# Streaming expert weights with 16 KB rows: two ring slots filled by one transfer

## The reference

```python
logits = (xf @ w_router) + b_router          # 264 tokens, 32 experts
top_v, top_e = lax.top_k(logits, 4)
gates = jax.nn.softmax(top_v, axis=-1)
# for the tokens xb of every expert e:
gu = xb @ w_e1[e] + b_e1[e]                  # w_e1[e]: 1024 x 2048
g, u = gu[:, :1024], gu[:, 1024:]
g = jnp.minimum(g, 7.0); u = jnp.clip(u, -7.0, 7.0)
h = (u + 1.0) * (g * jax.nn.sigmoid(1.702 * g))
rows = h @ w_e2[e] + b_e2[e]                 # w_e2[e]: 1024 x 1024
# out = sum over a token's four experts of gate * rows
```

## Time and profile before

| | |
|---|---|
| median of 3 runs | 1284.78 us (1280.65 to 1286.63) |
| the profiled execution | 1283.03 us, span 1281.3 us |
| mean granted TensorE clock | 0.974 |
| TensorE matmuls | 1172.0 us, 91% of the span |
| TensorE weight loads | 569.3 us, 44% |
| VectorE, ScalarE, GpSimd | 335.5, 181.5, 28.3 us |
| moved by DMA | 457.41 MB, mean 357 GB/s |
| expert transfers of 1 MiB | 380 |

### The profile page before, as it was taken

How to read it: one execution, slowest core, us unless ns; L and a number is a source line. 1 busy time by engine, 2 the same in 40 slices (tenths; PEclk the granted TensorE clock), 3 DMA queues, 4 the chain that set the end, 5 groups by cost and what they waited for, 6 DMA issues and landing times.

```text
span 1281.3 us, 15118 instructions
## 1 busy us (share of the span) xinstructions
PE 1172.0 (91%) x5539; PEld 569.3 (44%) x5539; DVE 335.5 (26%) x805; ACT 181.5 (14%) x350; POOL 28.3 (2%) x58
## 2 busy tenths in 40 slices
PE   5999999699899999999999999989998999999996
PEld 3888888578333433333333333333332333232332
DVE  2397620815112121220212121212112021212123
ACT  3111512313001101111110101011110101010102
POOL 5000000200000000000000000000000000000000
PEclk9999999898889999999999999999999999999999
DMA  8449333796589999999999999999999999999994
GB/s 238 150 157 349 124 129 132 276 402 230 197 352 407 421 422 421 421 421 421 421 421 421 421 422 421 421 422 421 421 421 420 421 421 421 422 421 421 422 420 181
DMA packets 92470, 457.41 MB, mean 357 GB/s; under 512 B 7811, under 2 KB 36699, under 8 KB 43797
## 3 DMA queue, kind: packets, MB, share of 16 engines
q1 hardware_dynamic: 90528, 452.31, 87.9%
q10 hardware_dynamic: 1085, 3.01, 0.6%
q0 software_dynamic: 832, 1.76, 0.5%
HBM read 453.71 MB, written 3.81 MB: 357 GB/s over the span
## 4 chain that ended last, share of the span: by engine, by line
PE 52%; DMA 23%; SPq 13%; DVE 6%; issue 3%; ACT 2%; ACTq 0%; POOL 0%; DVEq 0%; POOLq 0%
DMA ring<-in_w_e 23%; PE ps L1495 15%; PE ps L1515 13%; SPq L351 12%; PE ps L1209 12%; PE ps L1225 3%; DVE ring L928 2%; PE ps L1457 1%; PE ps L1466 1%; PE ps L1409 1%; PE ps L1505 1%; DVE mix L1079 1%; DVE mix L1076 1%; DVE mix L1082 1%; SPq L359 1%
## 5 line engine op out<-in xcount | busy, mean ns | idle before, releaser
L1495 PE MATMUL ps<-ring,mix 128*64 128x512 f32 x2016 | 456.5, 598 | 26.6 <-DMA ring<-in_w_e 25.2
L1495 PEld LDWEIGHTS ps<-ring,mix 128*64 128x64 f32 x2016 | 134.2, 136 | 333.3 <-issue 237.5
L1515 PE MATMUL ps<-ring,mix 128*64 128x512 f32 x1024 | 240.6, 624 | 22.0 <-issue 11.0
L1076 DVE TENSOR_SCALAR mix<-ps 128x512 f32<-128x512 f32 x32 | 22.1, 692 | 603.2 <-PE ps L1495 603.2
L1515 PEld LDWEIGHTS ps<-ring,mix 128*64 128x64 f32 x1024 | 81.0, 143 | 160.8 <-issue 146.7
L1209 PE MATMUL ps<-xn,ring 128*128 128x264 f32 x384 | 89.9, 398 | 4.5 <-DVE xn L760 4.5
L1209 PEld LDWEIGHTS ps<-xn,ring 128*128 128x128 f32 x384 | 75.4, 197 | 18.1 <-issue 4.6
L687 ACT ACTIVATE mix<-mix 128x512 f32<-128x512 f32 x32 | 20.1, 630 | 417.3 <-DVE mix L1076 417.3
L1466 PEld LDWEIGHTS ps<-mix 128*128 128x128 f32 x544 | 64.9, 196 | 14.4 <-issue 13.0
L697 ACT ACTIVATE mix<-ps 64x512 f32<-64x512 f32 x64 | 37.8, 591 | 233.7 <-PE ps L1515 233.3
L1466 PE MATMUL ps<-mix 128*128 128x128 f32 x544 | 69.5, 282 | 1.3 <-ACT rstd L669 1.3
(11 more groups left out here) (281 smaller groups left out, 574.9 us busy)
## 6 DMA issues: line engine op xcount, KB each, us to landing
ring<-in_w_e SPq DMA_DIRECT2D x380, 1024.0 KB, 24.8
ring<-in_w_in SPq DMA_DIRECT2D x8, 1024.0 KB, 16.0
ring<-in_cache_mem_k SPq DMA_DIRECT2D x8, 1024.0 KB, 4.8
ring<-in_cache_mem_v SPq DMA_DIRECT2D x8, 1024.0 KB, 8.4
ring<-in_w_k SPq DMA_DIRECT2D x4, 1024.0 KB, 8.9
ring<-in_w_v SPq DMA_DIRECT2D x4, 1024.0 KB, 12.6
ring<-in_w_out SPq DMA_DIRECT2D x4, 1024.0 KB, 12.7
ring<-in_w_q SPq DMA_DIRECT2D x4, 1024.0 KB, 11.9
```

Of the source, the lines that this page charges most:

```text
L1076: dve.tensor_scalar(g1, ps[0][:, :], LIMIT, None, ALU.min).then_inc(S["g_clamped"], 1)
L1495: m = pe.matmul(ps[gu][CAP * i:CAP * i + CAP, :], xeT[:, k, CAP * e2:CAP * e2 + CAP], g_u[gu][:, 512 * i:512 * i + 512], start=False, stop ...
L1515: m = pe.matmul(ps[3][CAP * i:CAP * i + CAP, :], hTv[:, k % 4, CAP * (k // 4):CAP * (k // 4) + CAP], ring[:, s, D * (k % 2) + 512 * i:D * ...
```

## The change

One constant is new: `DEAL[k]` is the set of contraction rows that belong to block k, every second row of a group of 256. `fill` now takes two neighbouring slots s and s + 1 with one transfer of 2 MiB. For w_e1, partition p gets rows 256 (s/2) + 2p and the one after it, 16 KB in one piece; for w_e2, it gets four rows of 4 KB, again 16 KB. Only the even slots' semaphores are used, and the wait in front of a transfer is for the later of the two slots to be free. The head pieces take the rows of `DEAL[k]`, still in pieces of 4 KB. On TensorE, `gather` and L1559 read the token matrix at every second column, `turn_h` reads `hh` at every fourth, `up` waits for the even slot's semaphore, and `down` waits once for two slots.

```diff
+DEAL = [slice(2 * P * (_k // 2) + _k % 2, 2 * P * (_k // 2 + 1), 2) for _k in range(KD)]
 
                 sp.wait_ge(S["freed"], free)
                 if s < W_SLOTS:
-                    src = a["w_e1"][0][bass.ds(e, 1), s * P:(s + 1) * P, :].rearrange("o p c -> p (o c)")
-                    dst = ring[:, s, :]
+                    src = a["w_e1"][0][bass.ds(e, 1), s * P:(s + 2) * P, :].rearrange("o (p t) c -> p (o t c)", t=2)
                 else:
                     j = s - W_SLOTS
-                    src = a["w_e2"][0][bass.ds(e, 1), j * 2 * P:(j + 1) * 2 * P, :].rearrange(
-                        "o (p t) c -> p (o t c)", t=2)
-                    dst = ring[:, s, :]
+                    src = a["w_e2"][0][bass.ds(e, 1), j * 2 * P:(j + 2) * 2 * P, :].rearrange(
+                        "o (p t) c -> p (o t c)", t=4)
+                dst = ring[:, s:s + 2, :].rearrange("p s c -> p (s c)")
                 sp.dma_start(dst, src).then_inc(filled[s], 16)
 
             def expert(e, b, first=0):
 
-                for s in range(first, RING):
-                    fill(e, s, RING * b + freed_after(MOE0 + s - RING))
+                for s in range(first, RING, 2):
+                    fill(e, s, RING * b + freed_after(MOE0 + s + 1 - RING))
...
-                    sp.dma_start(head[k][gu], a["w_e1"][0, 0, k * P:(k + 1) * P, D * gu:D * gu + D]).then_inc(S["head_filled"], 16)
+                    sp.dma_start(head[k][gu], a["w_e1"][0, 0, DEAL[k], D * gu:D * gu + D]).then_inc(S["head_filled"], 16)
...
-            for s in range(HEAD_SLOTS, W_SLOTS):
-                fill(1, s, freed_after(MOE0 + 2 * (s - HEAD_SLOTS)))
+            for s in range(HEAD_SLOTS, W_SLOTS, 2):
+                fill(1, s, freed_after(MOE0 + 2 * (s + 1 - HEAD_SLOTS)))
...
-                            m = pe.matmul(ps[4 + i][:, P * (k % 4):P * (k % 4) + P], xnt[:, t, k * P:(k + 1) * P],
+                            m = pe.matmul(ps[4 + i][:, P * (k % 4):P * (k % 4) + P], xnt[:, t, DEAL[k]],
...
-                        pe.wait_ge(filled[k], 16 * b + 16 * (fills_before(MOE0 + k) - 1))
+                        pe.wait_ge(filled[k - k % 2], 16 * b + 16 * (fills_before(MOE0 + k) - 1))
                     else:
-                        pe.wait_ge(filled[k], 16 * b + 16 * fills_before(MOE0 + k))
+                        pe.wait_ge(filled[k - k % 2], 16 * b + 16 * fills_before(MOE0 + k))
...
-                    c = 2 * P * (j // 2) + j % 2
-                    m = pe.transpose(ps[2][:, j * P:(j + 1) * P], hh[:, c:c + 2 * P - 1:2], ident[:, :])
+                    m = pe.transpose(ps[2][:, j * P:(j + 1) * P], hh[:, j:4 * P:4], ident[:, :])
...
-                    if k % 2 == 0:
+                    if k % 4 == 0:
                         pe.wait_ge(filled[s], 16 * b + 16 * fills_before(MOE0 + s))
...
-                m = pe.transpose(ps[2][:, NB * k:NB * k + NB], xnt[0:NB, 2, k * P:(k + 1) * P], ident[0:NB, 0:NB])
+                m = pe.transpose(ps[2][:, NB * k:NB * k + NB], xnt[0:NB, 2, DEAL[k]], ident[0:NB, 0:NB])
```

More of the change, by code:

```diff
@@ L371, in _ @@
             fill_head(2)
-            for s in range(HEAD_SLOTS, W_SLOTS):
-                fill(0, s, freed_after(MOE0 + s - RING))
+            for s in range(HEAD_SLOTS, W_SLOTS, 2):
+                fill(0, s, freed_after(MOE0 + s + 1 - RING))
             bias(0)
[L375 to L378, removed]
+            for s in range(0, HEAD_SLOTS, 2):
+                fill(1, s, freed_after(MOE0 + s + 1 - RING))
+            for s in range(W_SLOTS, RING, 2):
+                fill(0, s, freed_after(MOE0 + s + 1 - RING))
             sp.wait_ge(S["tm_turned"], 6)
```

## The result

The changed kernel takes 1273.97 us (median of 6 runs, 1273.03 to 1274.95), the kernel before 1283.24 us beside it (6 runs, 1280.65 to 1286.63). The ratio is 0.9927, with a 95% interval from 0.9909 to 0.9944: 9.3 us less. The forecast was 1277.0, in a range from 1271 to 1290.

A forecast was written before the change was run, and what follows sets the result against it. The prediction took the DMA engines' rate as the bound from about 397 to 1253 us. Its terms, -12.8 + 1.7 + 1.8 + 1.5 = -7.8 us, gave 1275.2 profiled and, with 1.75 added, a median of 1277.0 us, range 1271 to 1290.

The forecast's parts named there:

- What bounds the kernel: Weight stream in the expert loop: the DMA engines' rate, near 421 GB/s, is the bound from about 397 to 1253 us.
- The packets, -12.8: Weight stream from 393 to 1253 us: 16 KB packets shorten a pair of experts from 59.86 to 58.97 us, -12.8 us.
- The straight line: Packet time per DMA engine, from 1, 4 and 8 KB rows: about 9 ns per packet plus 36.9 ns per 1000 B.
- The start, +1.7: Issue of expert 3's slot 0, where the stream becomes unbroken: it also waits for slot 1, one slot of up, +1.7 us.
- The end, +1.8: Last pair of slots, 6 and 7: they land together and 16 matmuls follow instead of 8, +1.8 us.
- Strided weight reads, +1.5: TensorE before 391 us: 64 gather loads at 15 ns and 8 turn_h transposes at 67 ns more, +1.5 us (bounds 0 and 5.4).
- the term put at nothing: The eight transposes of the sample rows at L1559, now read strided: taken to cost nothing.
- The offset to the median: From the profiled execution, 1275.2 us forecast, to the median of runs: 1.75 us added, giving 1277.0.
- No gain in rate: Rival for the stream: 16 KB rows are cut or loss is per byte; only delays of +5.0 remain, 1290 us; chance 0.14.
- A part of the gain: Rival for the stream: by the 417 GB/s row of 4 KB cache loads, only -3.5 us gained, 1286 us; chance 0.12.
- TensorE takes over: Rival for the loop: strided reads use up TensorE's cover and it sets the pace, 1291 us; chance 0.08.
- The forecast's point, 2.3 us a pair: Loop: extra TensorE work per pair that uses up its cover of some 35 us before the last up slot.

The follow-up runs named there:

- rows_4k: Changed kernel with each row of its slot pairs cut into 4 KB packets, two 1 MiB transfers per pair, both waited for; 1314.02 us, ratio 1.0246.
- quads_32k: Changed kernel with w_e1 in 32 KB packets, four slots per 4 MiB transfer, rows dealt in fours; 1285.35 us, ratio 1.0022.
- quads_sorted: Changed kernel with w_e1 in 32 KB packets, four slots per transfer, and tokens written once in dealt order so gather reads unstrided; 1275.37 us, ratio 0.9945.
- pairs_8k: Changed kernel's 2 MiB transfers and pairwise waits, but 8 KB packets and the earlier kernel's undealt rows and reads; 1286.25 us, ratio 1.0025.
- edges: Changed kernel with single-slot transfers for slots 0 to 3 of expert 3 and 6, 7 of expert 31; 1271.07 us, ratio 0.9911.
- edges_both: Changed kernel with single slots for expert 2's 8 to 11, expert 3's 0 to 3, and 6, 7 of experts 30 and 31; 1272.52 us, ratio 0.9918.
- end_both: Changed kernel with single-slot transfers only at the end, slots 6 and 7 of experts 30 and 31; 1272.87 us, ratio 0.9925.
- dealt_8k: Kernel before, one slot per transfer and 8 KB packets, but rows and token columns dealt as in the change; 1283.09 us, ratio 1.0008.
- pe_plus4: Changed kernel with the first half of gather done three times instead of once in every pair of the loop; 1291.84 us, ratio 1.0073.

## Why the prediction was right, and where not

**What bounds the kernel: right.** The plateau is the DMA engines', and both kernels follow it to the last landing. Every microsecond of the gain lies between the first unbroken issue and that landing.

**The packets, -12.8: right, -12.6 measured.** The straight line held at the two lengths that were not in it, and at 4 KB, where its point came from a stretch of 5 us. Per packet and DMA engine, by the distance between pairs of experts:

| packet | from | ns | line |
|---|---|---|---|
| 4 KB | `rows_4k`, 61.76 us / 384 | 160.8 | 160 |
| 8 KB | before, 59.86 / 192 | 311.8 | 312 |
| 16 KB | changed, 58.97 / 96 | 614.3 | 614 |
| 32 KB | `quads_32k`, (58.74 - 19.66) / 32 | 1221 | 1219 |

The 32 KB row rests on one pair of experts; by the 21 experts of `quads_sorted` it is (58.67 - 19.66) / 32 = 1219. What a packet loses is a fixed 9 to 10 ns. The step to 16 KB took half of it, 0.9 us a pair; the step to 32 KB for two thirds of the bytes brings 0.2 to 0.3 us a pair more. The Trainium skill (DMA: Bandwidth & Descriptors, "Why small descriptors are slow") gives 3 cycles beside one per 32 B and would have made it 0.6%; the measured 1.5% decides.

**The start, +1.7: the issue is late by that, but undoing it gives back less.** In `pairs_8k`, which has the waits alone, and in the changed kernel the issue of expert 3's slot 0 comes 3.8 us behind the start of up at L1495 instead of 2.05: 1.7. In `pairs_8k` the delay reaches the end of the stream in full: from the issue (391.91) to the last landing (1253.90) it takes 861.99 us, the kernel before 861.96. The prediction named this one issue. The pair before it, expert 2's slots 8 and 9, is late as well (382.88 for 380.92), and I wrote that the earlier fills cost nothing. In `edges` the named issue alone came 1.9 us earlier and the landings only 0.4; with both places split, in `edges_both`, it was 0.3 us of landing, or 1.0 us counted in bytes. So the size fits, and through which of these waits it comes about is not shown.

**The end, +1.8: right, +1.7** from the last landing to the end. Here too undoing the wait gives back only 0.8, since the wait before it is uncovered (`end_both`).

**Strided weight reads, +1.5: mis-sized, 0.6 measured.** This is the step that failed: the term is the stretch from the sample rows' transposes to expert 2's up, 75.25 and 75.27 us with strided reads, 74.67 and 74.64 without (see `dealt_8k`). I took 15 ns for each gather load and 67 for each of turn_h, and nothing for the transposes of the sample rows. Measured: gather 196 for 192 ns, half a gather 1.89 for 1.79 us in the chain, and turn_h at every fourth element 210 ns where it was 207 at every second:

```profile
L1504 PEld LDWEIGHTS ps<-ident,mix x128: 195/210/226, 339.7 to 1249.0; 128*128 128x128 f32 x128
```

Most of the 0.6 us is in the term put at nothing. The sample rows' eight transposes took 1.14 us for 0.68 in the chain, and their loads, before and then changed, both at a granted clock of 1.00:

```profile
L1559 PEld LDWEIGHTS ps<-ident,mix x8: 135/137/138, 314.6 to 315.0; 8*128 8x128 f32 x8
```

```profile
L1558 PEld LDWEIGHTS ps<-ident,mix x8: 192/218/218, 313.7 to 314.5; 8*128 8x128 f32 x8
```

One line reads the same rows once unstrided and once at every second element, so a step of two does cost a transpose's load some 80 ns, which the comparison of two different lines in the earlier trace rows could only suggest. The errors were to carry that surcharge over to gather, whose loads are of another kind, and to let it grow with the step. 140 ns unstrided, 207 at two and 210 at four is no straight line, and gather, which is no transpose, has 192, 196 and 330 ns at one, two and four. One rule for both kinds does not come out of these rows. Of the rule in the Trainium skill (SBUF — State Buffer, the note on 16-byte lines) that a line needs two hits for full bandwidth, gather's loads agree (two is nearly free, four is dear), those of the transposes don't in either step.

**The offset to the median.** The forecast added 1.75 us, by which the profiled execution of before stood under its median. Three further runs brought that median to 1283.24, and the changed kernel's profiled execution is 0.35 us under its own: 1.4 us of the 3 by which 1277.0 was too high. The other 1.6 stand between the profiled executions (1275.2 forecast, 1273.62 measured). 0.9 are the strides, and the packets gave 0.2 less than forecast. Another 0.9 are luck, as far as these executions show: in the changed kernel's execution the sample rows' transposes began at 313.71, before at 314.61, ahead of anything that the change touches on TensorE; in `pairs_8k` it was 313.49, in `dealt_8k` 314.50. So the start's +1.4 in the table is -0.9, +0.6 and +1.7.

**The rivals.** No gain in rate: out, the packets are 16 KB and the plateau 428 GB/s. A part of the gain: out by the same row and by `rows_4k`. TensorE takes over: out here, since the strides cost TensorE some 0.1 us a pair (55.56 for 55.45), but the mechanism is real. `quads_32k` met it with gather's loads at every fourth element, and `pe_plus4` with plain extra work. The forecast's point, 2.3 us a pair, is somewhat generous: with 1.9 us a pair TensorE already ends the chain, though what that costs is at the edge of what the runs can tell.

## What to carry to other kernels

When a stream keeps the DMA engines full, read the time per packet at two or three row lengths that the trace already has. If they lie on a line, the intercept is what longer rows save (here -12.8 us forecast, -12.6 measured); take stretches much longer than 5 us for it. Deal the contraction rows so that neighbours in memory land in one partition; here that cost the matmuls next to nothing with the weights read at every second element, and a lot at every fourth. Coarser transfers wait for coarser pieces, at the start and the end of the stream: set their price against the saving, because the next doubling saves half as much and waits twice as long.

## What the runs showed of the hardware that I had not expected

SP's issue of a transfer grows long when many are queued, and the rows fit a wait for room by the number of transfers and not of packets. Line L351 between 630 and 1230 us, the kernel before, then `pairs_8k`, then the changed kernel (ns min/median/max):

```profile
L351 SPq DMA_DIRECT2D ring<-in_w_e x241: 332/1924/4602, 628.4 to 1227.4; - x121
```

```profile
L351 SPq DMA_DIRECT2D ring<-in_w_e x120: 372/373/385, 637.4 to 1227.8; - x120
```

```profile
L351 SPq DMA_DIRECT2D ring<-in_w_e x122: 332/333/337, 635.4 to 1228.3; - x122
```

With some ten transfers of 1 MiB in flight an issue takes 1.9 us. With five of 2 MiB it takes 0.37 us, although in `pairs_8k` the same number of 8 KB packets is queued. While the queue was still short, the kernel before had it at 332 to 337 ns too (404 to 450 us). It cost nothing that shows (59.86 us a pair with it, 59.90 without), but it fills the chain of the kernel before with SP's links, which look like a cause and vanish in `pairs_8k` without any gain.
